# GpSimdE instead of VectorE makes the low half of the last two weight sums of each seven-product unit

## The reference

```python
def swiglu(x, w1, w3, w2):
    return (jax.nn.silu(x @ w1) * (x @ w3)) @ w2

x = x + 0.5 * swiglu(rms_norm(x, g_ffn1), w1_ffn1, w3_ffn1, w2_ffn1)
z = rms_norm(x, g_mix) @ w_in + b_in
# windowed attention and a spatial gate on z, then
x = x + jnp.concatenate([attn_out, gm_out], axis=-1) @ w_out + b_out
x = x + 0.5 * swiglu(rms_norm(x, g_ffn2), w1_ffn2, w3_ffn2, w2_ffn2)
x = x + gate * (ple @ w_ple_proj)
```

## Time and profile before

| | us |
|---|---|
| median of 3 runs | 968.97 (968.1 to 968.98) |
| the profiled execution: span from first to last instruction | 965.8 |
| TensorE busy (matmuls) | 953.1 (99%) |
| VectorE busy | 676.0 (70%) |
| ScalarE busy | 456.9 (47%) |
| GpSimdE busy | 225.3 (23%) |

### The profile page before, as it was taken

The page is one execution under the profiler, slowest core; times in us unless marked ns, Lnnn a source line. Parts: engine busy times, 40 slices in busy tenths (PEclk is TensorE's granted clock), DMA queues, the critical chain, the costliest instruction groups (busy, mean ns, idle before and its releaser), DMA issues.

```text
span 965.8 us, 19305 instructions
## 1 busy us (share of the span) xinstructions
PE 953.1 (99%) x7942; PEld 941.7 (98%) x7942; DVE 676.0 (70%) x1078; ACT 456.9 (47%) x750; POOL 225.3 (23%) x136
## 2 busy tenths in 40 slices
PE   7999999999999999999999999999999999999997
PEld 7999999999999999899999999999999999999997
DVE  6999568757678563557974499767766768855576
ACT  7645325533534444565545465434443443534243
POOL 0211111311111226300218412112311101114621
PEclk9999999999999999999999999999999999999999
DMA  8931524153143327312133783243324315235302
GB/s 242 176 95 48 164 70 117 53 156 89 44 134 108 99 77 210 80 45 67 45 87 101 137 170 110 82 116 98 99 85 127 94 57 143 67 99 163 89 23 89
DMA packets 190098, 100.33 MB, mean 104 GB/s; under 512 B 12986, under 2 KB 187412, under 8 KB 189996
## 3 DMA queue, kind: packets, MB, share of 16 engines
q1 hardware_dynamic: 176612, 90.27, 33.0%
q0 software_dynamic: 9360, 4.72, 3.9%
q10 hardware_dynamic: 4040, 4.12, 1.4%
HBM read 96.54 MB, written 3.59 MB: 104 GB/s over the span
## 4 chain that ended last, share of the span: by engine, by line
PE 90%; DVE 5%; ACT 2%; issue 1%; DMA 1%; SPq 0%; ACTq 0%; DVEq 0%
PE ps L1801 48%; PE ps L1879 37%; PE ps L2233 2%; PE ps L1835 2%; DMA x_rows<-in_x_prompt_dram 1%; DVE w_lo L1499 1%; PE ps L2135 0%; PE ps L2106 0%; DVE tt L1517 0%; DVE tt L1510 0%; DVE probs L1542 0%; ACT w_hi L744 0%; ACT tt L957 0%; PE ps L2257 0%; DVE ab L1394 0%
## 5 line engine op out<-in xcount | busy, mean ns | idle before, releaser
L1879 PE MATMUL ps<-xo_lo,w_hi 128*128 128x260 f32 x1008 | 284.7, 282 | 0.0
L1879 PE MATMUL ps<-xo_hi,w_lo 128*128 128x260 f32 x1008 | 284.4, 282 | 0.0
L1879 PE MATMUL ps<-xo_hi,w_hi 128*128 128x260 f32 x1008 | 284.1, 282 | 0.0
L1801 PE MATMUL ps<-h_hi,w_hi 128*128 128x260 f32 x960 | 194.6, 284 | 0.7 <-DVE x L1410 0.7
L1801 PE MATMUL ps<-h_hi,w_lo 128*128 128x260 f32 x960 | 193.0, 283 | 0.0
L1801 PE MATMUL ps<-h_lo,w_hi 128*128 128x260 f32 x960 | 192.9, 282 | 0.0
L1879 PEld LDWEIGHTS ps<-xo_hi,w_lo 128*128 128x128 f32 x1008 | 189.8, 188 | 0.0
L1879 PEld LDWEIGHTS ps<-xo_lo,w_hi 128*128 128x128 f32 x1008 | 189.7, 188 | 0.0
L1879 PEld LDWEIGHTS ps<-xo_hi,w_hi 128*128 128x128 f32 x1008 | 189.6, 188 | 0.0
L1801 PEld LDWEIGHTS ps<-h_hi,w_hi 128*128 128x128 f32 x960 | 147.5, 188 | 1.2 <-issue 1.0
L1801 PEld LDWEIGHTS ps<-h_lo,w_hi 128*128 128x128 f32 x960 | 148.2, 188 | 0.0
(11 more groups left out here) (286 smaller groups left out, 1447.4 us busy)
## 6 DMA issues: line engine op xcount, KB each, us to landing
w_raw<-in_w_ffn_dram SPq DMA_DIRECT2D x88, 256.0 KB, 3.0
w_a<-in_w_ffn_dram SPq DMA_DIRECT2D x36, 512.0 KB, 4.7
w_raw<-in_w_ffn_dram SPq DMA_DIRECT2D x48, 384.0 KB, 3.2
w_raw<-in_w_ffn_dram SPq DMA_DIRECT2D x16, 512.0 KB, 6.0
w_raw<-in_w_in_dram SPq DMA_DIRECT2D x10, 512.0 KB, 4.0
w_lo<-in_w_ffn_dram POOLq DMA_DIRECT2D x9, 512.0 KB, 7.6
w_raw<-in_w_ple_gate_dram SPq DMA_DIRECT2D x8, 512.0 KB, 3.6
x_rows<-in_x_prompt_dram SPq DMA_DIRECT2D x8, 256.0 KB, 6.3
```

The lines of the kernel that those rows point to most:

```text
L1801: ins = pe.matmul(ps[:, bank + step * h, 0:HALF], w[:, c, w0:w0 + P], m_[:, sk, h * HALF:(h + 1) * HALF], start=(first and n == 0), stop=( ...
L1879: ins = pe.matmul(ps[:, b, 0:Q], w[:, c, k * P:(k + 1) * P], m_[:, op, k, :], start=(first and k == 0 and n == 0), stop=(k == 3 and n == 2 ...
```

## The change

The step `w_lo_24` moves, at its place in the list, from VectorE to GpSimdE, where it stands ahead of the `a22` low half. It gets a semaphore of its own, and the products of `s2` and `s4` wait for that one. There are 36 such steps, 18 in each network.

```diff
+        unit_lo24 = sem("unit_lo24")
...
+                    elif kind == "w_lo_24":
+                        j, = arg
+                        g = N_UNIT * s + j
+                        pool.wait_ge(unit_hi, 4 * g + 3)
+                        nc.gpsimd.tensor_tensor(w_cells(wl, s, j, "s2", 2), w_cells(w_raw, s, j, "s2", 2),
+                                                w_cells(wh, s, j, "s2", 2).bitcast(F32),
+                                                ALU.subtract).then_inc(unit_lo24, 1)
...
-                    elif kind in ("w_lo_a", "w_lo_13", "w_lo_24"):
+                    elif kind in ("w_lo_a", "w_lo_13"):
                         j, = arg
-                        i = ("w_lo_a", "w_lo_13", "w_lo_24").index(kind)
-                        name = ("a11", "s1", "s2")[i]
+                        i = ("w_lo_a", "w_lo_13").index(kind)
+                        name = ("a11", "s1")[i]
                         dve.wait_ge(unit_hi, 4 * (N_UNIT * s + j) + i + 1)
...
                 if name == "a22":
                     pe.wait_ge(unit_lo22, g + 1)
+                elif name in ("s2", "s4"):
+                    pe.wait_ge(unit_lo24, g + 1)
                 else:
-                    pe.wait_ge(unit_lo, 3 * g + {"a11": 1, "a12": 1, "s1": 2, "s3": 2, "s2": 3, "s4": 3}[name])
+                    pe.wait_ge(unit_lo, 2 * g + (2 if name in ("s1", "s3") else 1))
```

## The result

The changed kernel takes 975.31 us (974.76 to 976.55) against 968.54 us before, measured again beside it: a ratio of 1.0075, 95% interval 1.0061 to 1.0089 (the two medians by themselves give 1.0070, inside that interval). It is slower, by 6.8 us; 974.6 us had been forecast. The span of the profiled execution went from 965.8 to 973.6 us, so 7.8 us longer.

What follows compares the result with a forecast made beforehand. TensorE, busy 99% of the span, was taken as the bound. Span 965.8 plus 2.8 us of waits in each of two networks gives 971.4, plus 3.2 from span to median 974.6 us; 8-in-10 range 969.2 to 979.

Steps and rivals of the forecast that it cites:

- The bound: Whole kernel: TensorE is busy 99% of the span, so a shorter VectorE can win at most 0.7 us.
- Turns, in order of asking: VectorE instructions with both operands in SBUF alternate with GpSimdE's steps, first come first; PSUM-reading `comb`s are untouched.
- Price of the moved step: On GpSimdE, each of 36 subtractions of 128x1024 takes 2.40 us while it holds its turn.
- less about 0.14 us: VectorE loses all of GpSimdE's turn except about 0.14 us, so 2.26 us per moved step.
- Where: Units 0 to 3: waits before product 5 of unit 2 (1.0 us), its product 4 (1.4), unit 0's product 4 (0 to 0.8).
- The term: TensorE's wait in units 0 to 3 of each network, 2.2 to 3.2 us, taken as 2.8.
- the race around unit 0: Whether GpSimdE asks before VectorE changes instruction; decides if at most 1.0 us hides beside unit 0's three `comb`s.
- Unit 8: At its start, VectorE loses up to 1.5 us more; 0 to 0.4 us for TensorE, left at nothing.
- The sum: Span 965.8 plus 2.8 us for each of two networks gives 971.4; with 3.2 added, 974.6 us.
- 3.2 had been carried over: Whole kernel: the distance between profiled span and median time, 3.2 us, added to the forecast span.
- What was to be seen after: VectorE's busy time falls under 42 us, GpSimdE's new line has a median over 2.40, TensorE's waits name VectorE.
- Nowhere else: TensorE's waits, about 1 us each, come only in the first three units of each network.

Runs made afterwards that it cites:

- e4: Changed kernel, but GpSimdE's moved subtraction replaced by a 128x1024 copy of the high half over the low half; 967.61 us in one run, span 965.8.
- e7: Kernel before the change, with the `a22` low half also moved from GpSimdE to VectorE; ratio to before 0.9998, span 965.7 us.
- e8: Changed kernel, but GpSimdE's moved subtraction replaced by two 128x512 memsets writing zeros over the low halves; 967.25 us in one run, span 965.5.
- e5: Kernel before the change, VectorE's work kept, plus two 128x512 GpSimdE subtractions per preparation whose result nobody reads; ratio to before 1.0160, span 980.6 us.
- e3: Changed kernel, but GpSimdE's moved step also waits for the high half of `a22`; ratio to before 1.0039, span 969.3 us.
- e6: Changed kernel, but GpSimdE's moved step made as two 128x512 subtractions instead of one 128x1024; ratio to before 1.0045, span 970.3 us.
- e2_late: Changed kernel, but the step is GpSimdE's only for units 4 to 17, VectorE's for units 0 to 3; ratio to before 1.0010, span 966.9 us.

## Why the prediction was right

- **The bound.** TensorE had no wait in the units that VectorE could shorten, 0.7 us in all before. Confirmed from the other side: e4, e7 and e8 give VectorE room and the spans are 965.8, 965.7 and 965.5.
- **Turns, in order of asking.** Confirmed by e5 (turns without relief, 14.8 us lost), by e3 and e6 (same work, other order or size of turns, 3.8 and 3.3 us won back), and by the rows above.
- **Price of the moved step.** 2.40 us was taken; the median after is 2.42. Of a turn, "less about 0.14 us" was read too small: the earlier trace rows have 1.08 to 1.10 us lost for a step of 1.29, so 0.2 less, and the moved step holds VectorE off for 2.2 us (4.57 for 2.37) and not 2.26. VectorE's start of sums in unit 0 came 1.1 us late net, as worked out for one preparation.
- **Where.** Units 0 to 3: three waits, at the three products named, 0.9, 0.9 and 1.3 us for "0 to 0.8", "about 1.0" and "1.4". The term was 2.2 to 3.2 with 2.8 taken; 3.3 was measured, just outside. Two things made it so. One is what a wait costs TensorE beyond the wait, some 0.25 us three times, for which the sum had no term: the waits themselves are 2.5 us (0.89, 0.62, 1.03). The other is the race around unit 0, which left the `comb` of unit 2 3.5 us late, in the upper half of 2.85 to 3.85 (less the cover of 0.6 that is 2.9, within the term): GpSimdE asked less than 0.1 us before VectorE changed instruction. I had taken the middle of both outcomes though my own numbers had GpSimdE in first; e3_wait shows the other outcome.
- **Unit 8.** Put at 0 to 0.4 and taken at nothing; it was 0.5 us a network, 1.1 us in all (e2_late alone). The sum lacks as much here as in units 0 to 3.
- **The sum.** 5.6 us forecast, 7.8 in the span, 6.8 between the medians. The distance from span to median was 1.7 us after, where 3.2 had been carried over. In every execution whose own span is on record the time lies 1.7 to 2.0 us above it; the 3.2 set the median of three runs beside the span of a quicker one. With 1.7 the sum gives 973.1, 2.2 us under the 975.31. That 974.6 came within 0.7 is in good part luck: the stall was put too low and the distance too high.
- **What was to be seen after.** VectorE's time fell less than 42 us (6.7), GpSimdE's new line has a median above 2.40 (2.42), the waits name L1365 and L1388. "Nowhere else" was wrong: unit 8 is there, and waits "in units 4 to 17" stood among the signs that the prediction is wrong. It is 1.1 of the 7.8 us, from the same cause.

Open is what the 0.25 us after a wait consists of, and whether e3 and e6 together would bring the loss to nothing; no run shows either.

## What to carry to other kernels

Before moving an elementwise step from VectorE to an idle GpSimdE, compare two numbers: what VectorE gives up (1.15 us here) and how long GpSimdE holds it off (2.2 us); where the first is smaller, VectorE is the poorer for each instruction with two SBUF operands that it could have run. Then look at the stretches, not at the share: 70% busy over the kernel hid two stretches at 98%, and they paid six sevenths of the bill. If such a step must go to GpSimdE, put it beside VectorE's PSUM reads, or in short pieces. When it asks matters as much: asking later helped here because VectorE's own low half then got in first.

## What was not expected

- Nothing in the first prediction had it that asking later is faster: one semaphore count more, 0.8 us later in unit 0, is worth 3.8 us, half of the loss.
- GpSimdE's copy of 128x1024 takes 1.04 us at its shortest and 1.11 in the median, the subtraction of the same size 2.40 at its shortest; in VectorE's turn it is 0.84 us for 2.2. The second operand costs more than the first, in GpSimdE's time and in VectorE's turn alike.
- Two VectorE sums in a row (L1340 at 177.68 and L1343 at 179.25 after the change, 1.65 and 1.78 us for 0.68) each lost a turn to GpSimdE's queue of three, where before only the first lost 0.8. Unit 8 loses another 3.3 us of turns at 182.53 and 187.03, as unit 0 does in all, so it loses 5.4 us, the most of any unit; that is why its room was not enough.
